# A two-layer trunk on one core: which product-key queries are computed ahead of the second attention, and where a second half's scores stand

## The reference, cut to what matters

```python
h = rmsnorm(x) * (1 + sc1) + sh1
x = x + g1 * mixer(h)                      # conv module, or attention
h = rmsnorm(x) * (1 + sc2) + sh2
q = (h @ w_q).reshape(T, 8, 2, 128)        # 8 heads, two half queries each
s = einsum('thcd,hcnd->thcn', q, sub_keys) # 128 scores for each half query
top_s, top_i = top_k(s, 16)                # 16 best of each half
cand = top_s[:, :, 0, :, None] + top_s[:, :, 1, None, :]
best_s, best_c = top_k(cand, 16)           # 16 best of the 256 sums
experts = i1 * 128 + i2                    # of the two key lists' indices
gates = softmax(best_s)
y = sum_k gelu(u_tab[experts] . h) * gates * v_tab[experts]
x = x + g2 * y
```

## Time and profile before

| | |
|---|---|
| runs of the kernel | 3181.22 us median of 3, from 3177.64 to 3181.43 |
| the profiled execution | 3174.62 us |
| its span, first to last instruction | 3172.9 us |
| mean granted TensorE clock | 0.969 of full |
| busy: TensorE, VectorE, ScalarE, GpSimd | 92%, 74%, 17%, 46% of the span |
| mean DMA rate | 302 GB/s |

### The profile page before, as it was taken

How to read it: one execution, slowest core, us unless ns; L and a number is a source line. 1 busy time by engine, 2 the same in 40 slices (tenths; PEclk the granted TensorE clock), 3 DMA queues, 4 the chain that set the end, 5 groups by cost and what they waited for, 6 DMA issues and landing times. The chain is left out here.

```text
span 3172.9 us, 45195 instructions
## 1 busy us (share of the span) xinstructions
PE 2911.0 (92%) x12846; PEld 2092.3 (66%) x12846; DVE 2347.8 (74%) x4952; ACT 538.4 (17%) x1366; POOL 1470.2 (46%) x1502
## 2 busy tenths in 40 slices
PE   6998988999999999999899988759999999999997
PEld 4786766777766665555587866657677666655554
DVE  2999799888888866666523664998887888667666
ACT  2122214300000000000232243134000000000001
POOL 0000355355555577777300210463655555777664
PEclk8998988999999999999999999979999999999999
DMA  7644355599999999999743322334999999999998
GB/s 287 239 159 181 123 179 188 206 410 401 410 409 405 405 409 410 410 410 410 271 142 117 133 80 80 107 100 174 410 409 408 402 408 404 410 410 410 410 410 323
DMA packets 242903, 957.20 MB, mean 302 GB/s; under 512 B 26954, under 2 KB 27130, under 8 KB 225147
## 3 DMA queue, kind: packets, MB, share of 16 engines
q0 software_dynamic: 147456, 536.94, 42.9%
q1 hardware_dynamic: 95354, 419.17, 34.4%
HBM read 953.90 MB, written 2.10 MB: 301 GB/s over the span
## 5 line engine op out<-in xcount | busy, mean ns | idle before, releaser
L873 PE MATMUL out_e<-weights,mod_rows 128*128 128x512 f32 x2048 | 932.7, 598 | 61.3 <-DVE mod_rows L1588 59.5
L864 PE MATMUL acc<-h_t,weights 128*128 128x256 f32 x4096 | 930.4, 380 | 0.0
L864 PEld LDWEIGHTS acc<-h_t,weights 128*128 128x128 f32 x4096 | 780.9, 191 | 218.9 <-issue 125.1
L484 POOL DMA_INDIRECT v_rows<-in_pk_v,idx_now x512 | 625.5, 1222 | 568.2 <-DVE mod_rows L1526 453.5
L1526 DVE SCALAR_TENSOR_TENSOR mod_rows<-v_rows,acts,mod_rows 128x1024 f32<-128x1024 f32 x512 | 657.6, 1284 | 206.6 <-DMA v_rows<-in_pk_v,idx_now 203.9
L478 POOL DMA_INDIRECT u_rows<-in_pk_u,idx_now x512 | 586.5, 1145 | 235.4 <-issue 145.2
L1509 DVE SCALAR_TENSOR_TENSOR u_rows<-u_rows,h_rows 128x1024 f32<-128x1024 f32 x512 | 625.5, 1222 | 86.2 <-DMA u_rows<-in_pk_u,idx_now 85.1
L873 PEld LDWEIGHTS out_e<-weights,mod_rows 128*128 128x128 f32 x2048 | 376.9, 190 | 468.5 <-issue 368.3
L510 POOL CAST top_f<-top_i 128x64 f32<-128x64 uint32 x32 | 7.6, 236 | 834.1 <-DVEq L1467 824.1
L1212 ACT ACTIVATE mod_rows<-acc 128x256 f32<-128x256 f32 x256 | 98.1, 383 | 1189.5 <-PE acc L864 1186.1
L575 PE MATMUL acc<-h_t,weights 128*128 128x256 f32 x1024 | 235.5, 390 | 15.8 <-ACT h_t L1013 6.9
(11 more groups left out here) (229 smaller groups left out, 2394.3 us busy)
## 6 DMA issues: line engine op xcount, KB each, us to landing
weights<-in_u_t SPq DMA_DIRECT2D x256, 512.0 KB, 6.7
weights<-in_pk_v SPq DMA_DIRECT2D x256, 512.0 KB, 6.7
weights<-in_pk SPq DMA_DIRECT2D x32, 1024.0 KB, 4.9
v_rows<-in_ada SPq DMA_DIRECT2D x30, 1024.0 KB, 6.7
weights<-in_w_qkv SPq DMA_DIRECT2D x24, 1024.0 KB, 4.8
weights<-in_w_in SPq DMA_DIRECT2D x16, 1024.0 KB, 8.4
weights<-in_ada SPq DMA_DIRECT2D x14, 1024.0 KB, 4.9
weights<-in_w_out SPq DMA_DIRECT2D x8, 1024.0 KB, 4.9
```

The lines of the kernel that those rows point to most:

```text
L484: nc.gpsimd.indirect_dma_start(v_rows[:, r % VR, :], None, a["pk_v"], bass.IndirectOffsetOnAxis(ap=idx_now[:, 1, par, r:r + 1], axis=0)).t ...
L864: last = nc.tensor.matmul(acc[s][:, 0:HALF], weights[:, s, k * P:(k + 1) * P], h_t[:, k, :], start=k == 0, stop=k == KB - 1)
L873: last = nc.tensor.matmul(out_e[2 * tt + c][:, :], e_act[:, s, tt * P:(tt + 1) * P], weights[:, s, D + c * 512:D + (c + 1) * 512], start=F ...
```

## The change

The first half of layer 1 now has seven query chunks (heads 0 to 6) with their scores ahead of the eight chunks of the second half's q, k and v. Chunk 7 takes the place behind the second attention that chunk 6 had, its scores stand behind the first projected chunk, and no query chunk or score of the first half is left between the projection and the norm, or behind the norm. VectorE ranks heads 0 to 6 ahead of the second attention and head 7 between the residual additions; `less_best(1, 0)` moves ahead of the last residual addition. Second halves, in both layers since `select` is shared, now issue `score(l, h, i)` right behind the chunk of head i.

```diff
--- before.py
+++ after.py
@@ -82,9 +82,9 @@
          [(c, 0, h, i) for c, h, k in (("out", 0, range(4)), ("pk", 0, range(FIRST)), ("out", 1, range(4)),
                                        ("pk", 0, range(FIRST, 8)), ("pk", 1, range(8))) for i in k] +
          [("qkv", 1, 1, i) for i in AHEAD] +
-         [(c, 1, h, i) for c, h, k in (("qkv", 0, QKV), ("out", 0, range(4)), ("qkv", 1, AMID), ("pk", 0, range(FIRST)),
-                                       ("qkv", 1, REST), ("pk", 0, (FIRST,)), ("out", 1, range(4)),
-                                       ("pk", 0, range(FIRST + 1, 8)), ("pk", 1, range(8))) for i in k])
+         [(c, 1, h, i) for c, h, k in (("qkv", 0, QKV), ("out", 0, range(4)), ("qkv", 1, AMID), ("pk", 0, range(7)),
+                                       ("qkv", 1, REST), ("pk", 0, (7,)), ("out", 1, range(4)), ("pk", 1, range(8)))
+          for i in k])
 NUMBER = {_c: _n for _n, _c in enumerate(CHAIN)}
 
 LATE = 12
@@ -685,7 +685,9 @@
                 for i in heads:
                     by_channel("pk", l, h, i)
                     beside("pk", l, h, i)
-                    if i != 1:
+                    if h:
+                        score(l, h, i)
+                    elif i != 1:
                         score(l, h, max(i - 1, 0))
                     if i in between:
                         between[i]()
@@ -811,7 +813,7 @@
                 for i in range(4):
                     by_token("out", 1, h, i, lambda k, tt: q_t[:, k, tt * P:(tt + 1) * P])
                     if h and i == 0:
-                        score(1, 0, FIRST)
+                        score(1, 0, PH - 1)
 
             def peer(l):
 
@@ -938,7 +940,6 @@
             normed_columns(0, 1, 1)
             score(0, 0, PH - 1)
             select(0, 1)
-            score(0, 1, PH - 1)
             for n in range(LATE):
                 pe.wait_ge(late_in[n % 2], 16 * (n // 2 + 1))
                 ada_chunk(ADA_CHUNKS - LATE + n, weights[:, n % 2, :], out_e[0], False).then_inc(late_used, 1)
@@ -958,19 +959,15 @@
             attention_out(0)
             project(1, 1, 1)
             norm(1, 0, 1, lambda: project(1, 1, 2))
-            select(1, 0, range(FIRST))
-            score(1, 0, FIRST - 1)
+            select(1, 0, range(PH - 1))
+            score(1, 0, PH - 2)
             for i in REST:
                 project(1, i % 4, i // 4)
             second_attention()
-            by_channel("pk", 1, 0, FIRST)
+            by_channel("pk", 1, 0, PH - 1)
             attention_out(1)
-            by_channel("pk", 1, 0, PH - 1)
             norm(1, 1, 1)
-            normed_columns(1, 1, 1)
-            score(1, 0, PH - 1)
             select(1, 1)
-            score(1, 1, PH - 1)
             peer(1)
 
         @block.scalar
@@ -1118,7 +1115,7 @@
                     nc.scalar.activation(q_t[:, pair, :], mid[0][:, 0:HALF], ACT.Copy).then_inc(o_ready, 1)
 
 
-                act.wait_ge(looked_up, PK[1, 0] + FIRST)
+                act.wait_ge(looked_up, PK[1, 0] + PH - 1)
                 sigmoids(0)
                 for pair in range(PAIRS):
                     if pair + 1 < PAIRS:
@@ -1140,11 +1137,14 @@
             def select(l, h, heads=range(PH), between={}):
                 for i in heads:
                     take_q(l, h, i)
-                    if i != 1:
+                    if h:
+                        take_scores(l, h, i)
+                    elif i != 1:
                         take_scores(l, h, max(i - 1, 0))
                     if i in between:
                         between[i]()
-                take_scores(l, h, heads[-1])
+                if not h:
+                    take_scores(l, h, heads[-1])
 
             def last_query():
                 take_q(0, 0, PH - 2)
@@ -1268,15 +1268,14 @@
             first_attention()
             squares(1, 0, 1)
             norm(1, 0, 1, lambda: (take(1, 1, 1), take(1, 1, 2)))
-            select(1, 0, range(FIRST))
+            select(1, 0, range(PH - 1))
             for i in REST:
                 take(1, i % 4, i // 4)
             second_attention()
-            take_q(1, 0, FIRST)
-            take_scores(1, 0, FIRST)
+            take_q(1, 0, PH - 1)
+            take_scores(1, 0, PH - 1)
             squares(1, 1, 1)
-            norm(1, 1, 1, lambda: take_q(1, 0, PH - 1))
-            take_scores(1, 0, PH - 1)
+            norm(1, 1, 1)
             select(1, 1, between={3: lambda: exps(1, 0)})
             peer(1)
 
@@ -1681,18 +1680,17 @@
             for i in range(4):
                 residual(1, 0, i)
             reciprocal_root(1, 0, 1)
-            for head in range(FIRST):
+            for head in range(PH - 1):
                 rank(1, 0, head)
 
-            mark_places(1, 0, FIRST - 1)
+            mark_places(1, 0, PH - 2)
             attention(1)
             residual(1, 1, 0)
-            rank(1, 0, FIRST, lambda: residual(1, 1, 1), True)
+            rank(1, 0, PH - 1, lambda: residual(1, 1, 1), True)
             residual(1, 1, 2)
+            less_best(1, 0)
             residual(1, 1, 3)
             reciprocal_root(1, 1, 1)
-            rank(1, 0, PH - 1)
-            less_best(1, 0)
             for head in range(PH):
                 rank(1, 1, head)
                 if head == 2:
```

## The result

The changed kernel took 3185.99 us (median of 20 runs, 3181.05 to 3190.42), the kernel before 3177.72 (median of 20, 3172.92 to 3183.0). The ratio is 1.0024 with a 95% interval of 1.0018 to 1.0031, so the change costs 7.6 us, between 5.7 and 9.9; forecast were 8.8. The two medians themselves lie 8.3 us apart. In absolute time the forecast of 3190.0 is 4.0 us high: the median of the three runs shown lay 3.5 us above that of twenty, and the forecast difference was 0.5 us more than that of the medians.

The account below looks back on a forecast made before the run. Expert-stage starts were taken to bound the kernel: layer 0's set by TensorE, layer 1's by VectorE. Terms 6.6 + 1.7 + 0.5 = 8.8 us on 3181.2 gave 3190.0 us, range 3182 to 3196.

Parts of the forecast that it names:

- Layer 0's term: Layer 0's second half: wider-spaced chunks delay TensorE's first gates, and the whole 6.6 us passes on; bounds 4.0 to 9.2.
- a cover: Start of layer 0's expert stage: VectorE's 2.73 us wait for the first gates hides none of the 6.6 us.
- the rival in which VectorE covers it: Layer 0: one-hot tiles set the pace, leaving only the 1.6 us column wait; total 3.8 us; chance 0.14.
- one slow landing: Layer 0's late chunk loads: one slow landing more or less on the chain moves the term by 2.6 us.
- Layer 1's term: Layer 1's second half: head 1's rank 1.70 us late plus 0.46 us for a residual addition, together 2.2 us.
- the residual addition beside the look-up: Layer 1's last residual addition, slowed beside GpSimd's look-up of head 7: 0.46 us on the path, 0 at least.
- The first chunk at half clock: Layer 1's first second-half chunk, after about 7.2 us of TensorE idle: 9.09 us, 2.02 more than 7.07.
- `less_best` fitted: Layer 1: `less_best`, 3.9 us, fits VectorE's 5.28 us wait for the last projected chunk, 1.4 us to spare.
- scores right behind the chunk decide head 1's rank: Layer 1's second half: head 1's scores, rankable at 2008.65, come after head 0's rank ends at 2008.09, so they decide.
- the attention's later start eats the gain: Layer 1: the 14.5 us leaving VectorE's path are eaten by a 7.8 us later attention and the cold chunk.
- The clock's part: Layer 1 behind the projection: idle TensorE halves its clock, making layer 1's term 2.2 us instead of 0.5.
- The sum: Whole kernel: 6.6 + 1.7 + 0.5 = 8.8 us slower, 3190.0 us; the forecast holds 0.70.

Follow-up runs that it names:

- the edit alone: Kernel before with each head's scores right behind its chunk in layer 0's second half, layer 1 as before: ratio 1.0028, +8.9 us (5 to 12).
- l1_seven: Kernel before with seven heads ahead of layer 1's attention, the eighth in its tail, every score product still one chunk late: 1.0021, +6.7 us (3.8 to 9.6).
- eight_ahead: Layer 1's part of the change alone, with all eight heads and `less_best` ahead of the second attention: 1.0009, +2.9 us against the kernel before.
- l1_all_warm: Layer 1's part of the change alone, plus 30 useless products between projection and norm: 0.9999, -0.3 us against the kernel before.
- l1_all: Changed kernel with layer 0's second half put back to the old order, so layer 1's part alone: 1.0004, +1.3 us (-1.6 to +4.1) against before.
- l1_scores: Kernel before with scores right behind each chunk in layer 1's second half only; measured twice: 0.9995, -1.6 us, and 0.9994, -1.9 us.
- best: Kernel before with layer 1's second-half scores right behind each chunk and layer 0's first gates ahead of the first table block: 0.9987, -4.1 us.

## Why the prediction was right

**Layer 0's term** was forecast at 6.6 us (4.0 to 9.2), and the mechanism is the one that the runs show. The eighth chunk stands 61.28 us behind the first, forecast 61.25. VectorE's wait, which I had weighed as a cover, passed the delay on: it grew from 2.73 to 8.04 us, and from the first gates to the end the stage took 78.88 us in both traces. The time of the edit alone, +8.9 us (5 to 12), leaves out the rival in which VectorE covers it (1.6). The columns made VectorE wait 2.17 us, where I had 1.6. That the shift in the changed kernel's own trace, 6.96 us, comes so near to 6.6 is luck in part, since 1.69 us of a slow first chunk and 1.35 us of a shorter way to the gates stand against each other. That way took 63.6 to 66.2 us in the traces, a spread of 2.6 us, the size that I had given to one slow landing; which landing makes it was not looked into.

**Layer 1's term** was forecast at 2.2. By the changed kernel's distances it is 7.80 - (35.82 - 29.90) + 0.56 = 2.4, the 0.56 being what lies between attention and transposes (111.81 against 111.25), which fits the residual addition beside the look-up (0.61 more, forecast 0.46). The first chunk at half clock took 9.29 and 10.17 us, forecast 9.09; 0.52 us of wait before head 1's rank, forecast 0.56; `less_best` fitted with 0.9 us left, forecast 1.4. The term's time, 1.3 us (-1.6 to +4.1), agrees. That scores right behind the chunk decide head 1's rank is shown by l1_seven. That the attention's later start eats the gain is shown by the 7.80 us in D1; eight_ahead agrees. The clock's part is shown in two traces by products that hold it up, 1.2 to 2.1 us and 0.9 us in D2. Behind 7.60 us of idle time the transposes took 1.97 us; behind a single gap of 3.59 us they took 1.09 to 1.17 us in seven traces and 1.52 in l1_all_warm. The section "Why this matters for your kernels" of the Trainium skill's page TensorE: Matmul & The Clock Gate warns that an idle gap of over about 3 us between bursts halves the clock. The trace agrees for the gap of 7.60 us, and does not for the single gap of 3.59 us.

**The sum**, 8.8, against 7.6 (5.7 to 9.9). The two parts measured alone give 8.9 + 1.3 = 10.2 us with some 4.5 us of uncertainty, so they add up within it.

**The profiled 11.8 us** are not the change's cost. Head 1's rank is 12.17 us later. Of this 5.63 are there when layer 1's first transposes start (1569.25 and 1574.88), 2.4 are layer 1's term, 1.61 are the slow chunk at 1763.98, and 2.49 lie in the first half's attention and projection. Of these 2.49, 1.84 are the four projected chunks there (128 instructions, in the same order in both programs): 29.73 us from 1715.72, at a granted clock of 0.94, where they took 27.89 from 1709.44, at 1.00. The 1.61 and the 1.84 us are the clock in work that the change does not touch; the other 0.65 of the 2.49 were not located. For the same reason head 1's rank came at 2019.12 and not near 2015.3, as forecast.

## What to carry to other kernels

Where a helper is shared, cost the edit at every place that calls it: here three quarters of the loss lay in layer 0, while most lines of the edit are about layer 1. Work moved ahead of a stage is free only if the engine that sets that stage's start has a gap there; a chunk moved out of a gap into a full queue costs its whole length, and leaves a gap whose half clock costs more. Before cashing in an engine's wait by moving work, look where the work lands: the 2.73 us at layer 0's gates came back as 2.50 us of waits behind the place it was moved to.

## What the runs showed of the hardware

The clock behind one and the same idle time came out differently from execution to execution. The first half's first chunk in layer 1, always behind 2.6 us of idle time, took 7.17 us in two traces (the kernel before and l1_all) and 8.55 to 8.86 in the twelve others. Layer 0's first chunk of the second half, always behind a score product that followed 2.55 us of idle time, took 7.07 us in seven traces and 8.76 in seven. From the attention's start to the transposes it took 111.3 us or 113.8 in kernels with the same instructions there (111.25 before, 113.81 in l1_scores, 111.26 in best), and from 50 to 75 us behind the attention's start the granted clock was 0.93 before and 0.80 in l1_scores. Together these three move a single execution by up to some 6 us (an estimate: 1.7 + 1.7 + 2.5), most of what this study had to measure. Distances between two rows inside one trace told apart terms that whole spans and times could not, but one distance in one trace is still one draw.
